# Splitting each weight chunk with one 2048-column instruction per engine instead of two of 1024

## What is computed

```python
# first block
proj = rms_norm(x, g_mix) @ w_in                 # 2048 x 9216
... stick-breaking attention, spatial gating ...
merged = sigmoid(gate_a) * (o @ w_oa) + sigmoid(gate_b) * (s @ w_ob)
x = x + merged @ w_out
x = x + square(relu(rms_norm(x, g_ff) @ w_ff1)) @ w_ff2     # d_ff 8192
# second block
mod = silu(c) @ ada_w + ada_b                    # on VectorE, beside the first block
p = modulate(rmsnorm(x, norm1_g), ...) @ w_in_2
... neighbourhood attention, Fourier mixing, long convolutions ...
x = x + g1 * (y @ w_out_2)
gate, up = split(modulate(rmsnorm(x, norm2_g), ...) @ ffn_w_up)
x = x + g2 * ((gelu(dwconv(gate)) * up) @ ffn_w_down)       # d_ff 5632
return rmsnorm(x, final_norm_g)
```

## Time and profile before

| | us |
|---|---|
| median of 3 runs | 2610.56 |
| the profiled execution | 2608.22 |
| its span | 2606.2 |
| PE busy in it | 2580.8 (99%) |
| DVE busy | 1906.9 (73%) |
| ACT busy | 1186.8 (46%) |
| the split on DVE (L946), 840 instructions | 1018.0 |
| the split on ACT (L510), 840 instructions | 888.2 |

### The profile page before, as it was taken

How to read it: one execution, slowest core, us unless ns; L and a number is a source line. 1 busy time by engine, 2 the same in 40 slices (tenths; PEclk the granted TensorE clock), 3 DMA queues, 4 the chain that set the end, 5 groups by cost and what they waited for, 6 DMA issues and landing times.

```text
span 2606.2 us, 50006 instructions
## 1 busy us (share of the span) xinstructions
PE 2580.8 (99%) x20962; PEld 2496.2 (96%) x20962; DVE 1906.9 (73%) x2444; ACT 1186.8 (46%) x1262; POOL 0.2 (0%) x4
## 2 busy tenths in 40 slices
PE   9999999999999999999999999999999999999998
PEld 9889999999999999999999899959999999999997
DVE  8878877887998888888893236766666666666667
ACT  7766564444644444444442234343444444444443
POOL 0000000000000000000000000000000000000000
PEclk9999999999999999999999999999999999999999
DMA  8766667767888888888773244423455555555553
GB/s 313 245 239 213 227 231 255 246 241 234 284 278 279 283 282 280 282 282 283 268 254 98 97 162 149 152 78 131 162 194 195 194 195 194 194 193 192 191 192 107
DMA packets 282440, 558.23 MB, mean 214 GB/s; under 512 B 10295, under 2 KB 16728, under 8 KB 281944
## 3 DMA queue, kind: packets, MB, share of 16 engines
q1 hardware_dynamic: 282120, 553.60, 63.0%
q10 hardware_dynamic: 144, 2.10, 0.2%
HBM read 553.56 MB, written 2.10 MB: 213 GB/s over the span
## 4 chain that ended last, share of the span: by engine, by line
PE 92%; DVE 5%; issue 1%; ACT 1%; DMA 0%; SPq 0%; DVEq 0%; ACTq 0%
PE PS L1723 79%; PE PS L1733 3%; PE PS L1735 3%; PE PS L1734 3%; DVE WL L946 1%; PE PS L2049 1%; DVE ada1c L1199 1%; PE PS L2060 1%; PE PS L1956 1%; PE PS L2067 1%; PE PS L1889 0%; DMA RAW<-in_w_in 0%; PE PS L1783 0%; ACT WH L510 0%; DVE X L1318 0%
## 5 line engine op out<-in xcount | busy, mean ns | idle before, releaser
L510 ACT ACTIVATE WH<-RAW 128x1024 fp32r<-128x1024 f32 x840 | 888.2, 1060 | 1292.8 <-PE PS L1723 1174.8
L946 DVE TENSOR_TENSOR WL<-RAW,WH 128x1024 fp32r<-128x1024 f32 x840 | 1018.0, 1223 | 605.5 <-ACT WH L510 597.6
L1723 PE MATMUL PS<-XL,WH 128*128 128x256 f32 x4288 | 664.6, 277 | 0.0
L1723 PE MATMUL PS<-XH,WH 128*128 128x256 f32 x3752 | 587.3, 279 | 1.7 <-DVE WL L946 1.7
L1723 PE MATMUL PS<-XH,WL 128*128 128x256 f32 x3752 | 580.1, 277 | 0.0
L1723 PEld LDWEIGHTS PS<-XL,WH 128*128 128x128 f32 x4288 | 569.4, 188 | 0.0
L1723 PEld LDWEIGHTS PS<-XH,WH 128*128 128x128 f32 x3752 | 499.3, 188 | 4.7 <-issue 2.9
L1723 PEld LDWEIGHTS PS<-XH,WL 128*128 128x128 f32 x3752 | 496.7, 188 | 0.0
L1723 PE MATMUL PS<-HH,WH 128*128 128x256 f32 x1728 | 269.0, 278 | 1.4 <-DVE FR L1305 0.8
L1723 PE MATMUL PS<-HH,WL 128*128 128x256 f32 x1728 | 267.5, 277 | 0.0
L1723 PE MATMUL PS<-HL,WH 128*128 128x256 f32 x1728 | 267.4, 277 | 0.0
(11 more groups left out here) (274 smaller groups left out, 1965.6 us busy)
## 6 DMA issues: line engine op xcount, KB each, us to landing
RAW<-in_w_ff SPq DMA_DIRECT2D x128, 1024.0 KB, 5.9
RAW<-in_w_in SPq DMA_DIRECT2D x111, 1024.0 KB, 5.2
RAW<-in_w_up SPq DMA_DIRECT2D x88, 1024.0 KB, 5.0
adab<-in_ada_w SPq DMA_DIRECT2D x128, 512.0 KB, 5.1
RAW<-in_w_down SPq DMA_DIRECT2D x44, 1024.0 KB, 5.0
ada1b<-in_ada_w SPq DMA_DIRECT2D x64, 512.0 KB, 6.1
RAW<-in_w_out SPq DMA_DIRECT2D x32, 1024.0 KB, 5.2
RAW<-in_w_oa SPq DMA_DIRECT2D x8, 1024.0 KB, 5.1
```

The lines of the kernel that those rows point to most:

```text
L510: A(WH[:, c.base % 2, hs], RAW[:, c.base % SLOTS, hs], ACT.Copy).then_inc(hi_done, 1)
L946: tt(WL[:, b, hs], RAW[:, c.base % SLOTS, hs], WH[:, b, hs].bitcast(f32), ALU.subtract)\
L1723: ins = MM(out[:, f, :], w[:, b, kk, f * P:(f + 1) * P], x, start=first and n == 0 and f % 2 == 0, stop=last and n == 2, skip_group_check= ...
```

## The change

`high(c)` and `low(c)` become one instruction of 2048 columns each for every chunk from 2 on. The ACT instruction waits for PE to have done both halves of chunk c-2 (`c.value(2, -2)`). DVE waits for the whole high part and has no wait on `pe_half` any more, since ACT's has covered it. `hi_done` and `lo_done` rise by 2 at once. Direct calls of `high_half` and `low_half` stay: on ACT for chunks 5 and 289, on DVE for 105 and 289. PE's program, with its waits for halves, the DMAs and all other work stay as they are and where they are.

```diff
             def high(c):
-                high_half(c, 0)
-                high_half(c, 1)
+                if not c.since(2):
+                    high_half(c, 0)
+                    high_half(c, 1)
+                    return
+                act.wait_ge(raw_in[c.base % SLOTS], c.turns(SLOTS, 1, 16))
+                act.wait_ge(pe_half, c.value(2, -2))
+                A(WH[:, c.base % 2], RAW[:, c.base % SLOTS], ACT.Copy).then_inc(hi_done, 2)
...
             def low(c):
-                low_half(c, 0)
-                low_half(c, 1)
+                if not c.since(2):
+                    low_half(c, 0)
+                    low_half(c, 1)
+                    return
+                dve.wait_ge(hi_done, c.value(2, 2))
+                tt(WL[:, c.base % 2], RAW[:, c.base % SLOTS], WH[:, c.base % 2].bitcast(f32), ALU.subtract)\
+                    .then_inc(lo_done, 2)
```

## The result

The changed kernel takes **2686.0 us** (median, 2680.9 to 2690.1) against 2610.9 us of the kernel before in the same runs: ratio 1.0289 [1.0277, 1.0302], slower. The forecast was 2655 with a range of 2636 to 2674. The direction and the paths came as forecast, but the loss is 75 us in place of 45, outside the range.

A forecast was written before the change was run, and what follows sets the result against it. PE was taken as the bound, with ACT and DVE running ahead; five terms of delay, 15.5 + 4.2 + 9.0 + 14.0 + 1.9 = 44.6 us, on the profiled 2608.22 gave 2652.8, plus 2.3 for the median: 2655, range 2636 to 2674.

The forecast's parts named there:

- (a): Rival for the whole kernel: no change, within 0.2% of 2610.6, 2611 us; chance 0.04.
- (b): Rival: faster, DVE gaining 0.065 us a chunk in all 104 chunks before the first feed-forward part, 2604 us; chance 0.03.
- 0.065 a chunk: DVE saving, one 2.285 us instruction for two taking 2.35; counts where DVE sets the pace, some 20 chunks, 1.3 us.
- Durations: Instructions of 2048 columns: 1.92 us on ACT and 2.285 on DVE, from lines through two widths each.
- (d): Rival: new instructions cost twice the present ones, 0.37 more on each path, 63 us in all, 2673 us; chance 0.10.
- (c): Rival: only the slot paths and half of the rest, as DVE catches up between places, 32 us, 2642; chance 0.25.
- Term 1: Second feed-forward part: PE waits for PSUM slots freed behind DVE's split, 0.74 late per pair, 1.48 a step, 15.5 us.
- if PE's own pace changes after each wait: Sign that the forecast is wrong: PE's own pace changing after each wait; no size given.
- Term 2: First feed-forward part: same slot path with `relu_scaled` at s = 5, 0.30 a step, 14 steps, 4.2 us.
- Term 3: Where DVE already sets the pace, chunks 2 to 10, 14, 18, 34 to 35: PE late, 9.0 us, bounds 4.2 and 13.
- term 4: Much DVE work beside one chunk, as `merge`, residual squares, context norm, chunk 277: PE late, 14.0 us, bounds 7 and 18.
- Term 5: Second norm window, chunk 290: the split ends later and delays a quarter of the activations behind it, 1.9 us.

The follow-up runs named there:

- Experiment 9: Kernel before, whole split only inside the two feed-forward parts away from norms, PSUM taken out ahead of DVE's split there: 2611.5 us, ratio 1.0006.
- experiment 2: Changed kernel with what takes products out of PSUM put ahead of DVE's split in both feed-forward parts: 2649.9 us, ratio 1.0158.
- experiment 5: Kernel before plus one unread 1024-column DVE instruction ahead of `down_out2` at s = 10 and 0, second feed-forward part: 2609.0 us, ratio 1.0000.
- experiment 6: Kernel before plus two unread 1024-column DVE instructions ahead of `down_out2` at s = 10 and 0, second feed-forward part: 2635.0 us, ratio 1.0099.
- experiment 7: Changed kernel with 16 matmuls into a free PSUM bank ahead of chunks 78, 86 and 90: 2676.7 us, ratio 1.0259.
- experiment 1: Kernel before with the whole split only from chunk 288 on, halves before that: 2635.7 us, ratio 1.0103.
- experiment 10: Kernel before, halves everywhere, with PSUM taken out ahead of DVE's split in both feed-forward parts: 2607.6 us, ratio 0.9994.
- experiment 8: Changed kernel with DVE's attention work of the second block put ahead of the split of its chunk: 2678.2 us, ratio 1.0264.

## Why the prediction was right in kind and wrong in size

- **What bounds the kernel.** Right: PE. 45 us less work on DVE and 78 on ACT bought nothing, and both rivals that lived on this, (a) no change and (b) faster, have fallen. Experiment 9 is the clearest: where the lead is long enough the larger instruction is worth 0, not its 0.065 a chunk. The Trainium skill (Perfetto Trace Analysis, Optimizing Scalar/DVE Operations) says that work on an unsaturated engine is better broken up if others have bubbles behind it; the times here agree (2610.9 for halves, 2686.0 for the whole).
- **Durations.** Right within 0.01, so rival (d) is wrong in its cause, though its 2673 lay nearer to the result. Rival (c), half of the rest, has fallen: measured is more than the sum, not less.
- **Term 1 (15.5; measured 23.1).** The path is right (experiments 2, 5 and 6). Two steps of its sum failed: "With the change ACT starts at the same 2027.95" and "DVE starts 0.03 later, as now". ACT's start is 0.08 later than that of the half, and DVE's start comes 0.10 behind ACT's end. So "each follows the one before 0.74 late: 1.48 a step" is 0.89 and 1.79, 3.1 us more in ten steps. The last four chunks add 1.4 and not 0.74. The slow pace, 3.8 us, had no term. The prediction named "if PE's own pace changes after each wait" as something that would make it wrong; PE's pace did change, but behind some waits only.
- **Term 2 (4.2).** One wait a step at s = 5, as forecast, but 0.50 and not 0.30, and in ten of the steps the slow pace with 0.22 more: 8.6 us from chunk 129 on. The 0.20 are ACT's and DVE's later starts, as in term 1, and 0.12 in place of 0.05 from DVE's end at 849.27 to PE's start. DVE and PE at chunk 137:

```profile
845.84 2.29 DVE L960 TENSOR_TENSOR WL<-RAW,WH 128x2048 fp32r<-128x2048 f32 x1 [1.82 <-ACT WH L519]
848.05 1.22 DVE L1315 SCALAR_TENSOR_TENSOR FR<-PS,rt 128x1024 f32<-128x1024 f32 x1
...
849.39 0.53 PEld L1733 LDWEIGHTS PS<-HH,WH 128*128 128x128 f32 x4 [0.43 <-issue]
```

- **Terms 3 and 4 (23.0).** Single places came out well: chunk 14 lost 2.00 (1.9 forecast), chunk 78 2.36 (2.1), chunk 277 1.12 (1.1). Missed: three falls of the clock behind the merges (5.1, of which experiment 7 won back 4.4), chunk 54 (2.0, which I read as the attention chain behind the later split, but didn't test), and smaller ones at chunks 106, 227, 230 and 280 (3.9 together). Chunks 91 to 96 ran at the slow pace (1.3), but the same stretch does so in experiments 1, 5 and 10, which leave it as it was. That places close together would share a delay, the reason for the lower bound of term 4, did not happen.
- **Term 5 (1.9).** 2.01, right.
- **No term at all:** the attention of the second block. It stands behind the split as `down_out2` does, and I had looked for this pattern in the feed-forward parts alone: 4.6 us, shown by experiment 8. The fourth fall of the clock, 1.7, which isn't shown to be the change's, and 2.0 behind the last chunk.

In one sentence: the sum took the hand-overs from the halves and had no term for PE's pace or clock, while the larger instructions each started 0.07 to 0.08 us later behind what releases them, some waits were followed by a slower pace, pauses of 1 to 2 us by 1.7 us more at half the clock, and the same path ran through the attention as well.

## What to carry to other kernels

A larger instruction on an engine that doesn't set the time saves nothing there, but it lengthens each path that runs through a double buffer or a PSUM slot. Write down for each such path what it has to spare (here 1.24 us) and compare it with what the new durations add (1.06 fits, 1.92 and 1.98 don't), for every kind of work that stands behind the instruction, not for the most frequent alone. If the larger instruction must be, put what frees a slot ahead of it on its engine: this alone turned the loss in the second feed-forward part from 23 us into 0. A path that is taken twenty times needs its small terms too: the 0.15 us that two later starts put on each turn came to 3 us here.

## What had not been expected of the hardware

- **Later starts of the larger instructions.** ACT's instruction of 2048 columns starts 0.395 us behind the start of the matmul that it waits for, its second half of 1024 0.313; DVE's starts 0.102 behind ACT's end, the halves 0.033. This holds in all the kernels here, each for the engine whose instruction is the larger. The cause stays open.
- **Taking up again after a wait.** The first and the second matmul lie 0.22 us apart rather than 0.113, seen at chunk 317 and at the other waits of the feed-forward parts. In the fill experiment it stands too (0.71 for four), though PE had worked until 0.19 before. It costs nothing there, since the first matmul starts with its weight load and not 0.11 behind it: a wait of 1.08 us in experiment 6 makes the next chunk 0.01 later than that.
- **A slower pace.** 0.1178 us from matmul to matmul in place of 0.1133 at the same granted clock, that is 5.65 us a chunk. In the second feed-forward part it is seen only in kernels in which PE waits there, elsewhere also without such a wait. There its stretches of four and more chunks end with s = 3. What starts it in one step and not in the next stays open.
- **Half the clock for 3.4 us.** It followed the pauses at chunks 78, 86 and 90 of the changed kernel (PE stood for about 2, 2 and 1 us), and filling them with matmuls kept the clock. It did not follow the pauses at chunks 14, 18 and 54 there, of 2 us, but did follow the one at 18 in experiment 2. It also comes where the code is that of the kernel before: ahead of chunk 40 in experiments 1, 6 and 9, ahead of chunk 234 in experiments 5 and 6, and at neither place in the trace of before. So a pause doesn't bring it on every time, and which ones do stays open.
